# Other queue for the small parameters, first weights first on SyncE, shorter products of zeros in a one-core hybrid layer

## What is computed

```python
z = rmsnorm(x, attn_norm_g) @ w_in            # 2048 -> 1024 q, 256 k, 256 v, 1024 u
q, k, v, u = split_projection(z)
attn = window_attention(rmsnorm(q), rmsnorm(k), v)   # window 128, sinks, ALiBi

dt = exp(log_dt)
A_bar = exp((A_re + i*A_im) * dt)             # 64 groups x 64 complex states
B_bar = (A_bar - 1) / A * B
h_t = A_bar * h_(t-1) + B_bar @ u_t           # the scan over tokens
y = real(C @ h) + D * u
g = gelu(y)
ssm = g * sigmoid(g @ w_glu + b_glu)

h = x + concat(rmsnorm(attn), rmsnorm(ssm)) @ w_out
y = h + square(relu(rmsnorm(h) @ w_mlp_up)) @ w_mlp_down   # 2048 -> 8192 -> 2048
```

## Time and profile before

| | us |
|---|---|
| median of three runs | 1173.73 |
| the three runs | 1173.34 to 1173.75 |
| profiled execution, its own time | 1173.36 |
| span of the profiled execution | 1171.6 |
| PE busy in it | 1164.3 |
| DVE busy | 752.5 |
| ACT busy | 429.3 |

### The profile page before, as it was taken

The page is one execution under the profiler, slowest core; times in us unless marked ns, Lnnn a source line. Parts: engine busy times, 40 slices in busy tenths (PEclk is TensorE's granted clock), DMA queues, the critical chain, the costliest instruction groups (busy, mean ns, idle before and its releaser), DMA issues.

```text
span 1171.6 us, 20365 instructions
## 1 busy us (share of the span) xinstructions
PE 1164.3 (99%) x8510; PEld 1100.7 (94%) x8510; DVE 752.5 (64%) x761; ACT 429.3 (37%) x520; POOL 140.3 (12%) x83
## 2 busy tenths in 40 slices
PE   9999999999999999999999999999999999999998
PEld 7676676899999999999999999999999999999998
DVE  7999989989775566544455545555654445555554
ACT  6110033885444333333334333333333332433331
POOL 0502603000000011000001000001100000100000
PEclk9999999999999999999999999999999999999999
DMA  7533334424554444544454454444455444445543
GB/s 293 189 126 108 130 110 156 158 101 157 192 170 165 162 162 144 199 162 165 169 171 144 163 186 170 165 162 162 144 178 182 164 172 167 145 163 183 172 166 117
DMA packets 55192, 190.29 MB, mean 162 GB/s; under 512 B 7864, under 2 KB 10168, under 8 KB 54712
## 3 DMA queue, kind: packets, MB, share of 16 engines
q1 hardware_dynamic: 54824, 188.79, 46.8%
q10 hardware_dynamic: 288, 0.30, 0.1%
HBM read 185.82 MB, written 5.28 MB: 163 GB/s over the span
## 4 chain that ended last, share of the span: by engine, by line
PE 95%; DVE 4%; issue 1%; ACT 0%; POOL 0%; DVEq 0%; POOLq 0%
PE psum L1405 94%; DVE states L967 1%; DVE states L770 0%; DVE out_turn L770 0%; PE psum L1541 0%; DVE out_turn L1009 0%; DVE s_head L1083 0%; DVE q_t L1027 0%; DVE w_lo L761 0%; ACT gate L631 0%; DVE u_t L1021 0%; ACT L553 0%; DVE mov_b L770 0%; DVE q_t L770 0%; DVE stat L1088 0%
## 5 line engine op out<-in xcount | busy, mean ns | idle before, releaser
L761 DVE TENSOR_TENSOR w_lo<-w_raw,w_hi 128x1024 fp32r<-128x1024 f32 x294 | 409.6, 1405 | 385.4 <-ACT w_hi L472 384.6
L1405 PE MATMUL psum<-mov_b,w_hi 128*128 128x288 f32 x2656 | 528.9, 295 | 0.4 <-ACT au L538 0.3
L472 ACT ACTIVATE w_hi<-w_raw 128x1024 fp32r<-128x1024 f32 x294 | 308.6, 1059 | 491.9 <-PE psum L1405 480.3
L1405 PEld LDWEIGHTS psum<-mov_b,w_hi 128*128 128x128 f32 x2656 | 424.8, 188 | 2.5 <-issue 1.0
L1405 PE MATMUL psum<-mov_a,w_hi 128*128 128x288 f32 x2048 | 406.6, 295 | 0.0
L1405 PE MATMUL psum<-mov_b,w_lo 128*128 128x288 f32 x1328 | 390.1, 294 | 0.0
L1405 PEld LDWEIGHTS psum<-mov_a,w_hi 128*128 128x128 f32 x2048 | 327.7, 188 | 0.1
L1405 PE MATMUL psum<-mov_a,w_lo 128*128 128x288 f32 x1024 | 300.7, 294 | 0.0
L1405 PEld LDWEIGHTS psum<-mov_b,w_lo 128*128 128x128 f32 x1328 | 250.6, 189 | 0.0
L1405 PEld LDWEIGHTS psum<-mov_a,w_lo 128*128 128x128 f32 x1024 | 193.3, 189 | 0.0
L1405 PE MATMUL psum<-x_g,w_raw 128*128 128x288 f32 x640 | 162.1, 411 | 1.6 <-DVE turn L770 1.6
(11 more groups left out here) (182 smaller groups left out, 490.6 us busy)
## 6 DMA issues: line engine op xcount, KB each, us to landing
w_raw<-in_w SPq DMA_DIRECT2D x335, 512.0 KB, 3.3
h_t<-in_x SPq DMA_DIRECT2D x3, 576.0 KB, 8.7
out_y<-h_t SPq DMA_DIRECT2D x3, 576.0 KB
b_w<-in_b SPq DMA_DIRECT2D x1, 1024.0 KB, 7.6
c_w<-in_c SPq DMA_DIRECT2D x1, 1024.0 KB, 7.8
k_cache<-in_kc SPq DMA_DIRECT2D x1, 1024.0 KB, 5.4
v_cache<-in_vc SPq DMA_DIRECT2D x1, 1024.0 KB, 5.8
out_kc<-in_kc SPq DMA_DIRECT2D x1, 992.0 KB
```

Of the source, the lines that this page charges most:

```text
L472: nc.scalar.activation(hi3[:, n % SLOTS, :], raw3[:, n % SLOTS, :], ACT.Copy) \
L761: nc.vector.tensor_tensor(lo3[:, n % SLOTS, :], raw3[:, n % SLOTS, :], hi3[:, n % SLOTS, :].bitcast(F32), ALU.subtract) \
L1405: return nc.tensor.matmul(out, lhs_t, rhs, start=start, stop=stop)
```

## The change

It does three things. The transfer of `small` moves from the head of SP's queue to the head of ACT's, so that SP's first transfer is the first half of the first weight step and ACT's order is `small`, x tile 0, x tile 1. The zeros in `mov_b` are 288 columns instead of 512. PE's products of zeros are 14 over 288 columns instead of 4 over 512 and 8 over 288. (Before the change ACT's queue already carried both x tiles.)

```diff
             first = SMALL["h0"].start
-            sp.dma_start(small[:, 0:first], ins["small"][:, 0:first]).then_inc(small_loaded, 16)
             sp.dma_start(raw4[:, 0, 0, :], ins["w"][0, :, 0:STEP_N]).then_inc(w_first, 16)
...
+            first = SMALL["h0"].start
+            act.dma_start(small[:, 0:first], ins["small"][:, 0:first]).then_inc(small_loaded, 16)
             act.dma_start(h_t[:, 0:TOK], ins["x"][:, 0:TOK]).then_inc(x_first, 16)
             act.dma_start(h_t[:, TOK:2 * TOK], ins["x"][:, TOK:2 * TOK]).then_inc(x_second, 16)
             act.wait_ge(small_loaded, 16)
...
-            nc.gpsimd.memset(mov_b[:, 8192:8704].bitcast(F32), 0.0).then_inc(warm_filled, 1)
+            nc.gpsimd.memset(mov_b[:, 8192:8192 + TOK].bitcast(F32), 0.0).then_inc(warm_filled, 1)
...
-            zeros = mov_b[:, 8192:8704]
-            for cols in 4 * [512] + 8 * [TOK]:
-                mm(banks(UNIT["rms_x"], 1, 512)[:, 0, 0:cols], zeros[:, 0:P], zeros[:, 0:cols])
+            zeros = mov_b[:, 8192:8192 + TOK]
+            for _ in range(14):
+                mm(banks(UNIT["rms_x"], 1)[:, 0, :], zeros[:, 0:P], zeros)
```

## The result

| | before | after |
|---|---|---|
| median, us | 1173.60 (9 runs, 1173.29 to 1173.78) | 1177.20 (9 runs, 1175.56 to 1177.86) |
| profiled execution, its own time | 1173.36 | 1177.86 |
| its span | 1171.6 | 1176.1 |
| ratio of the runs, after to before, as recorded | | 1.0025, 95% interval 1.0016 to 1.0033 |

The changed kernel is slower, by 3.6 us between the medians (a ratio of 1.0031, inside the interval; the recorded ratio is not formed from the medians alone). That is more than the 1175.1 I had forecast and above the range's upper end of 1176.2. The executions of the changed kernel do not scatter evenly: four lie at 1175.6 to 1176.0 and five at 1177.2 to 1177.9.

A forecast was written before the change was run, and what follows sets the result against it. PE, busy 1164.3 of 1171.6 us, was taken as the bound, with two lanes to its first pair at 37.49. The x tile 1 lane's 1.7 us gave 1173.36 + 1.7 = 1175.06, called 1175.1; range 1173.6 to 1176.2.

The forecast's parts named there:

- The term of 1.7 us for x tile 1: At the start, x tile 1 reaches ACT near 6.7 instead of 4.98, by packet count on the queues: 1.7 us later.
- DVE's lane: x tile 1, exp, table load, sine, DVE's 28 us, `au`, up to PE's first pair: moves from 37.49 to 39.19.
- from 37.49 on PE and DVE shift together: After the first pair, the delay carries through whole, including PE's 1.58 us wait for DVE at 139.62; nothing further added.
- Which lane binds: Of two lanes to PE's first pair at 37.49, the one through x tile 1 and DVE binds, by 0.1 us.
- The wait at 37.34: PE's 0.14 us break between first projection and the pairs needing `u_t` and `au`; named the place to look at.
- the 4096-byte packets: SP's second weight step, which x tile 1, third on ACT's queue, would meet; reason for taking 1.7 us, not 0.46.
- Rival D: x tile 1 lands at 7.3 or later, slowest DMA engine deciding: 1175.8 to 1176.6 us; chance 0.06.
- The parameters and x tile 0: At the start, parameters land 0.2 to 0.3 us later, covered by x tile 1; x tile 0 is seen at 5.5.
- rival C: PE rests 1.5 us at the start, its clock level rises at 11.0, PE's lane ends at 40.3: 1176.2 us; chance 0.12.
- PE's lane: PE's own products up to the first pair: end at 37.85, 0.45 us later than 37.4, so not binding.
- The rule on queues: Queues share 16 DMA engines, so the move saves 0.4 us of issue on SP, costs as much on ACT: 1173.8 us.

The follow-up runs named there:

- the sine first: Changed kernel with ACT's exp and sine of the recurrence ahead of the gain of x tile 1: 1175.80 us; with 28 products of zeros as well: 1175.03 us.
- the second trace: Changed kernel measured once more, unedited: median 1177.29 us of 11; the traced execution took 1176.02 us.
- the late split: 72 short products in two halves with output projection tile 3 between: on the kernel before 1174.48 us, on the changed kernel 1176.70 us.

## Why the prediction was wrong, point by point

Two steps of the prediction failed. The term of 1.7 us for x tile 1 was mis-sized: DVE's lane moved by 2.3 to 2.7. And "from 37.49 on PE and DVE shift together" put the rest of the kernel at nothing, where a fall of the clock cost another 1.56 us. The first alone gives 1175.7 to 1176.1, still in the range; the second takes the median out of it.

- **Which lane binds: right, in all traces of the changed order but the first and those with the sine first.** The wait at 37.34 was the place, DVE's 28.54 us moved whole, and the zeros alone were worth 0 (1173.68 for 1173.70). The direction, slower, was right too, but I held a change beyond 0.2% at 0.14.
- **The delay of x tile 1: right mechanism, mis-sized term.** I had 1.7 us, x tile 1 at ACT near 6.7. It was 7.72 in the first trace and 7.3 to 7.7 in most others, 2.3 to 2.7 later. The bytes were right: 1.44 MB counted, to be through by 6.3, and 1.49 MB had moved by 6.5. What failed is that I took all 432 packets of ACT's queue to be through once those bytes had moved. 408 were, and the last 24 took until between 7.2 and 7.4. From the last packet to ACT it took 0.3 to 0.5 us, for the 0.4 of the forecast. The reason that I gave for the size of the term, the 4096-byte packets, is open: with 2304-byte packets x tile 1 stayed at 7.64 in the one trace, and the times came down by 0.5.
- **Rival D: it happened at the start.** It had x tile 1 at 7.3 or later, by the slowest DMA engine, and a time of 1175.8 to 1176.6; the executions with clock 1.000 lie at 1175.6 to 1176.2 but for one at 1177.2. I gave it 0.06. My rows of before showed the bulk of a transfer and had hardly an end to show. That the slowest engine decides is likely here and not shown.
- **The parameters and x tile 0.** The parameters landed 0.6 to 1.2 later, not 0.2 to 0.3, which stayed covered by x tile 1. X tile 0 came at 6.24 in the first trace, for 5.5, and at 5.0 to 5.6 in the others. Its sum had a slip: the 0.78 MB count SP's small packets as full ones; by the count of 128 per transfer that I used for x tile 1 it is 0.72, some 0.2 us less.
- **The clock at the start (rival C): it happened.** PE rested 2.05 us, and the level rose 3.9 us behind the first real product at 10.8; I had priced it at 4.9 us and given it 0.12. PE's lane came to 40.48, a third of a us behind DVE's. In the second trace it rose near 9.5 and did not bind. The Trainium skill, "TensorE: Matmul & The Clock Gate", section "Part 1: The HAM clock gate", says that the low level is the default and that activity releases it; the trace agrees (6.2 behind zeros without a rest, 10.8 behind a rest).
- **What was not in the sum: the fall near 256.** The trace of before shows a granted clock of 1.00 there, and its three times (and the six beside the result) lay within 0.5 us, so nothing priced it. It cost 1.56 us in the first trace. Of the changed kernel's 20 executions 11 have a lower mean clock, ten of them at 1177.29 to 1178.29, and thereby the median sits in the upper group. The executions with clock 1.000 (median 1176.08 in the second measurement) would have been within the range, by 0.1 us.
- **The rule on queues.** By the rule of the Trainium skill, "DMA: Bandwidth & Descriptors", section "Issuing engines are not separate DMA queues", the sum was 1173.8; the measurement decides against that sum. Here the third transfer of ACT's queue landed 5.9 to 6.0 us behind its issue, where the second had taken 3.8, so the move cost far more than the time of an issue.

The sum, with what was measured: 1173.6 + 2.5 (DVE's lane, up to 3.0 where PE's rest binds) + 1.6 where the clock falls = 1176.1 or 1177.7; the two groups are at 1176.0 and 1177.8.

## What to carry to other kernels

Before a transfer is moved to the head of another queue, follow what is behind it there to the first work that has no slack, and count the landing to the last packet, not to the bulk (here 24 of 432 packets came up to 0.9 us behind the rest). Where two lanes meet within 0.1 us, as here, shortening one of them is worth nothing and a delay of either is paid nearly whole. A change that delays a sequence can come with a loss far behind it: compare the granted clock over the whole trace, look for runs of short products, and time enough executions to see two groups if there are two.

## What the hardware showed that I had not expected

The granted clock fell to 0.50 for some 3.4 us with PE busy for every microsecond before it, behind a run of 72 short products. In the kernel before the mean clock is lower too in 23 of 108 executions, 20 of them slower by some 1.6 us, and neither its trace nor its first nine times showed it. The third transfer on ACT's queue landed near 7.6 us in one trace each with 144 KB, with 90.5 KB, and with packets of 2304 in place of 4096 bytes on the other queue. No version beat the kernel before: the late split takes its falls away, worth some 1.6 us in every fifth execution, and costs 0.9 in all of them.
